# 44 unit-matrix products on TensorE in the routing of a two-block network, and the last norm computed half by half on three engines

## The reference

```python
logits = jnp.einsum('bsd,de->bse', h, w_router).astype(jnp.float32)
aff = jax.nn.softmax(logits, axis=-1)
gate, idx = lax.top_k(aff.transpose(0, 2, 1), cap)      # cap = 128
xe = jax.vmap(lambda hb, ib: hb[ib])(h, idx)
...
```

```python
h = h + jnp.einsum('bsf,fd->bsd', jax.nn.silu(gate) * up, w_down[l])
return rms_norm_2(h, final_norm_w)
```

## Time and profile before

| | us |
|---|---|
| median of 3 runs | 3355.08 |
| lowest and highest | 3353.43, 3356.0 |
| the profiled execution's own time | 3356.99 |
| its span from first to last instruction | 3355.2 |
| TensorE matmuls busy | 3210.2 (96%) |
| VectorE busy | 2716.5 (81%) |
| ScalarE busy | 1782.5 (53%) |
| GpSimd busy | 692.0 (21%) |
| mean granted TensorE clock | 0.985 |

### The profile page before, as it was taken

How to read it: one execution, slowest core, us unless ns; L and a number is a source line. 1 busy time by engine, 2 the same in 40 slices (tenths; PEclk the granted TensorE clock), 3 DMA queues, 4 the chain that set the end, 5 groups by cost and what they waited for, 6 DMA issues and landing times. The chain is left out here.

```text
span 3355.2 us, 43403 instructions
## 1 busy us (share of the span) xinstructions
PE 3210.2 (96%) x15284; PEld 2590.3 (77%) x15284; DVE 2716.5 (81%) x2579; ACT 1782.5 (53%) x1911; POOL 692.0 (21%) x551
## 2 busy tenths in 40 slices
PE   7999996999999999999699999999998999999998
PEld 4859874888888785897488888888777878888786
DVE  7988887999989798888789888886744598888667
ACT  4254534887887524544378888863233353334223
POOL 0213100111111020320011111104453033233233
PEclk9999997999999999999899999999999999999999
DMA  5120165999999412005499999962110434444953
GB/s 201 38 96 16 36 214 217 394 409 404 410 403 410 181 51 87 22 8 192 184 377 397 395 393 396 391 261 82 47 38 16 154 113 151 142 166 148 372 233 137
DMA packets 143517, 703.06 MB, mean 210 GB/s; under 512 B 19376, under 2 KB 28080, under 8 KB 90672
## 3 DMA queue, kind: packets, MB, share of 16 engines
q1 hardware_dynamic: 132240, 664.65, 51.3%
q0 software_dynamic: 8928, 32.51, 3.6%
q10 hardware_dynamic: 2240, 4.46, 0.3%
HBM read 608.75 MB, written 85.46 MB: 207 GB/s over the span
## 5 line engine op out<-in xcount | busy, mean ns | idle before, releaser
L2212 DVE TENSOR_TENSOR ex_lo_layer<-mix_layer,ex_hi_layer 128x2048 fp32r<-128x2048 f32 x128 | 291.6, 2289 | 23.0 <-ACT ex_hi_layer L2140 21.3
L2212 DVE TENSOR_TENSOR ex_lo<-mix,ex_hi 128x2048 fp32r<-128x2048 f32 x128 | 289.5, 2285 | 12.5 <-ACT ex_hi L2140 10.8
L2140 ACT CAST ex_hi<-mix 128x2048 fp32r<-128x2048 f32 x126 | 239.8, 1912 | 77.3 <-DMA mix<-w_experts_dram 33.5
L2140 ACT CAST ex_hi_layer<-mix_layer 128x2048 fp32r<-128x2048 f32 x126 | 240.6, 1911 | 65.2 <-PE psum L2054 50.9
L3199 PE MATMUL psum<-ff_rest,w_hi 128*128 128x512 f32 x776 | 241.2, 392 | 8.6 <-DVE ff_ev L3477 2.8
L2052 PE MATMUL psum<-ex_hi_layer,xe_hi_layer 128*128 128x512 f32 x512 | 201.4, 393 | 1.0 <-DVE xe_lo_layer L2217 1.0
L2052 PE MATMUL psum<-ex_hi,xe_hi 128*128 128x512 f32 x512 | 201.3, 393 | 1.0 <-DVE xe_lo L2217 1.0
L2054 PE MATMUL psum<-ex_hi_layer,xe_lo_layer 128*128 128x512 f32 x512 | 200.1, 391 | 0.0
L2054 PE MATMUL psum<-ex_hi,xe_lo 128*128 128x512 f32 x512 | 200.1, 391 | 0.0
L2053 PE MATMUL psum<-ex_lo,xe_hi 128*128 128x512 f32 x512 | 199.8, 390 | 0.0
L2053 PE MATMUL psum<-ex_lo_layer,xe_hi_layer 128*128 128x512 f32 x512 | 199.8, 390 | 0.0
(11 more groups left out here) (800 smaller groups left out, 8822.2 us busy)
## 6 DMA issues: line engine op xcount, KB each, us to landing
mix<-w_experts_dram SPq DMA_DIRECT2D x128, 1024.0 KB, 12.1
mix_layer<-w_experts_dram SPq DMA_DIRECT2D x128, 1024.0 KB, 7.1
first_w<-w_experts_dram SPq DMA_DIRECT2D x64, 1024.0 KB, 9.3
hid_rows<-x SPq DMA_DIRECT2D x71, 512.0 KB, 3.7
ex_raw<-w_experts_dram SPq DMA_DIRECT2D x32, 1024.0 KB, 10.8
ex_raw_layer<-w_experts_dram SPq DMA_DIRECT2D x32, 1024.0 KB, 7.5
first_w<-w_in_dram SPq DMA_DIRECT2D x42, 512.0 KB, 3.3
ff_rest<-hid_rows SPq DMA_DIRECT2D x13, 1536.0 KB, 14.4
```

The costliest lines, as they stand in the source:

```text
L2140: act.copy(hi[j % PARTS][:], raw[j % RAW][:]).then_inc(w_hi, 1)
L2212: dve.tensor_tensor(lo[j % PARTS][:], raw[j % RAW][:], hi[j % PARTS][:].bitcast(F32), ALU.subtract).then_inc(w_lo, 1)
```

## The change

In `route`, TensorE gets 44 products of the unit matrix into bank 5 behind the last transpose of the rows and ahead of the wait for `place_done`. In the last stage the results `u2` and `u3` of the last unit go to PSUM banks 2 and 3. ScalarE multiplies tiles 0, 1 and the first half of tile 2 with the gain early; tile 7 is squared in two halves, the second first. TensorE finishes the sum of the first half before it begins the second. ScalarE writes the inverse of each half twice, into PSUM and into `sq_sum`. VectorE multiplies 5 tiles of the first half and 6 of the second, GpSimd the 3 and 2 others, and SP writes them out in an order that interleaves both.

```diff
+GAINED_TILES = (3, 2)
...
                                 mm = pe.transpose(banks(2 + 4 * b)[:, k * P:(k + 1) * P], h[:, k, blk * P:(blk + 1) * P], ident)
                             mm.then_inc(row_turned[b], 1)
+                        keep_busy(pe, 5, 44)
                         pe.wait_ge(place_done, 4)
...
+                def u2_of(n):
+                    return bank(2) if n == n_units - 1 else u2_row
+                def u3_of(n):
+                    return bank(3) if n == n_units - 1 else u3_row
...
                     @block.sync
-                            for k in range(DT):
-                                sp.wait_ge(normed, DT * half + k + 1)
+                            gained = GAINED_TILES[half]
+                            own = list(range(gained, DT))
+                            order = [k for n in range(len(own)) for k in own[n:n + 1] + ([n // 2] if n % 2 and n // 2 < gained else [])]
+                            order += [k for k in range(gained) if k not in order]
+                            for k in order:
+                                if k < gained:
+                                    sp.wait_ge(normed_too, half * GAINED_TILES[0] + k + 1)
+                                else:
+                                    sp.wait_ge(normed, half * (DT - GAINED_TILES[0]) + k - gained + 1)
                                 sp.dma_start(out[k * P:(k + 1) * P, at], x[:, k, at]).then_inc(written, 16)
...
                     @block.gpsimd
                         for tile in (DT - 4, DT - 3):
                             add_square(pool, tile)
+                        pool.wait_ge(out_gained, 3)
+                        for half, at in enumerate(halves):
+                            pool.wait_ge(inverted_too, half + 1)
+                            for k in range(GAINED_TILES[half]):
+                                pool.tensor_tensor(x[:, k, at], x[:, k, at], sq_sum[:, at], ALU.mult).then_inc(normed_too, 1)
...
                     @block.tensor
                         pe.wait_ge(sq_added, DT - 3)
-                        for half in range(2):
-                            pe.matmul(bank(sum_bank + half), ones, sq_sum[:, half_of(half)], start=True, stop=False)
+                        pe.matmul(bank(sum_bank), ones, sq_sum[:, first_half], start=True, stop=False)
                         pe.wait_ge(sq_done, DT - 1)
                         pe.matmul(bank(sum_bank), ones, square_of(DT - 2)[:, first_half], start=False, stop=False)
-                        pe.wait_ge(sq_done, DT)
+                        pe.wait_ge(sq_done, DT + 1)
                         pe.matmul(bank(sum_bank), ones, square_of(DT - 1)[:, first_half], start=False, stop=True).then_inc(r["summed"], 1)
+                        pe.matmul(bank(sum_bank + 1), ones, sq_sum[:, second_half], start=True, stop=False)
                         pe.matmul(bank(sum_bank + 1), ones, square_of(DT - 1)[:, second_half], start=False, stop=False)
-                        pe.wait_ge(sq_done, DT + 1)
+                        pe.wait_ge(sq_done, DT + 2)
                         pe.matmul(bank(sum_bank + 1), ones, square_of(DT - 2)[:, second_half], start=False, stop=True).then_inc(r["summed"], 1)
...
                     @block.scalar
+                            if n == n_units - 1:
+                                act.wait_ge(sq_done, 3)
+                                for k, at in ((0, slice(0, S)), (1, slice(0, S)), (2, first_half)):
+                                    act.activation(x[:, k, at], x[:, k, at], ACT.Copy, scale=out_gain[:, k:k + 1]).then_inc(out_gained, 1)
...
+                        act.wait_ge(dn_done, dn_at(n, "x2"))
+                        square(DT - 1, (second_half,), 1)
                         act.wait_ge(dn_done, dn_at(n, "x21"))
-                        square(DT - 1, (slice(0, S),), 1)
+                        square(DT - 1, (first_half,), 1)
                         act.wait_ge(dn_done, dn_at(n, "x12"))
                         square(DT - 2, (second_half,), 1)
-                        inverse_norms(act, r, sum_bank, sq_sum)
+                        for half, at in enumerate(halves):
+                            act.wait_ge(r["summed"], half + 1)
+                            act.activation(sq_sum[:, at], bank(sum_bank + half), ACT.Ln, bias=EPS, scale=1.0 / D).then_inc(r["logged"], 1)
+                            act.wait_ge(r["logged"], half + 1)
+                            act.activation(bank(sum_bank + half), sq_sum[:, at], ACT.Exp, scale=-0.5).then_inc(r["inverted"], 1)
+                            act.wait_ge(r["inverted"], half + 1)
+                            act.activation(sq_sum[:, at], sq_sum[:, at], ACT.Exp, scale=-0.5).then_inc(inverted_too, 1)
...
                     @block.vector
-                            dve.tensor_tensor(u2, bank(4 * (n % 2) + 1), p1, ALU.add)...
+                            if n == n_units - 1:
+                                dve.wait_ge(dn_done, dn_at(n - 1, "x12"))
+                            dve.tensor_tensor(u2_of(n), bank(4 * (n % 2) + 1), p1, ALU.add)...
...
-                        for half in range(2):
-                            at = half_of(half)
+                        for half, at in enumerate(halves):
                             dve.wait_ge(r["inverted"], half + 1)
-                            for k in range(DT):
-                                dve.scalar_tensor_tensor(out=x[:, k, at], in0=x[:, k, at], scalar=out_gain[:, k:k + 1], in1=sq_sum[:, at],
+                            for k in range(GAINED_TILES[half], DT):
+                                dve.scalar_tensor_tensor(out=x[:, k, at], in0=x[:, k, at], scalar=out_gain[:, k:k + 1], in1=bank(sum_bank + half),
```

More of the change, by code:

```diff
@@ L2937, in mix_and_feed_forward @@
                 so = split_tensors("so", DT, ctx, parts)
-                p1, u3, sil1, u2 = (ev[:, i, :] for i in range(4))
+                p1, u3_row, sil1, u2_row = (ev[:, i, :] for i in range(4))
+                def u2_of(n):
+                    return bank(2) if n == n_units - 1 else u2_row
+                def u3_of(n):
+                    return bank(3) if n == n_units - 1 else u3_row
                 sil = ev[:, 2:4, :].rearrange("p a n -> p (a n)")
@@ L2955, in mix_and_feed_forward @@
                 normed, written = sem("ff_normed"), sem("ff_written")
+                out_gained, inverted_too, normed_too = (sem("ff_" + n) for n in ("out_gained", "inverted_too", "normed_too"))
                 slot_in = [sem(f"ff_slot_in{i}") for i in range(SLOTS)]
@@ L3311, in gate_2 @@
                             act.wait_ge(ev_done, ev_at(n, "g2s"))
-                            act.activation(u2, u2, ACT.Silu).then_inc(silu2, 1)
+                            act.activation(u2_row, u2_row, ACT.Silu).then_inc(silu2, 1)
                         def block_hi(g):
@@ L3476, in take_u2 @@
                                 dve.wait_ge(dn_done, dn_at(n - 1, "u12"))
-                            dve.tensor_tensor(u2, bank(4 * (n % 2) + 1), p1, ALU.add).then_inc(ev_done if n < FFT else dn_done, 1)
+                            if n == n_units - 1:
+                                dve.wait_ge(dn_done, dn_at(n - 1, "x12"))
+                            dve.tensor_tensor(u2_of(n), bank(4 * (n % 2) + 1), p1, ALU.add).then_inc(ev_done if n < FFT else dn_done, 1)
                         def take_u3(n):
@@ L3484, in take_u3 @@
                                 dve.wait_ge(dn_done, dn_at(n - 1, "x2"))
-                            dve.tensor_tensor(u3, bank(4 * (n % 2) + 1), p1, ALU.add).then_inc(ev_done if n < FFT else dn_done, 1)
+                            dve.tensor_tensor(u3_of(n), bank(4 * (n % 2) + 1), p1, ALU.add).then_inc(ev_done if n < FFT else dn_done, 1)
                         def gate_in(n):
@@ L3500, in up_second @@
                             dve.wait_ge(ev_done, ev_at(n, "u3"))
-                            dve.tensor_tensor(hid[n % 2][:, second_half], bank(4 * (n % 2) + 2), u3, ALU.add).then_inc(ev_done, 1)
+                            dve.tensor_tensor(hid[n % 2][:, second_half], bank(4 * (n % 2) + 2), u3_row, ALU.add).then_inc(ev_done, 1)
                         def up_first(n):
                             dve.wait_ge(prod, prod_at(n, 5))
-                            dve.tensor_tensor(hid[n % 2][:, first_half], u3, bank(4 * (n % 2) + 3), ALU.subtract).then_inc(ev_done, 1)
+                            dve.tensor_tensor(hid[n % 2][:, first_half], u3_row, bank(4 * (n % 2) + 3), ALU.subtract).then_inc(ev_done, 1)
                             dve.wait_ge(ev_done, ev_at(n, "c21"))
@@ L3511, in gate_in_2 @@
                             dve.wait_ge(ev_done, ev_at(n, "u2"))
-                            dve.tensor_tensor(u2, bank(4 * (n % 2) + 2), u2, ALU.add).then_inc(ev_done, 1)
+                            dve.tensor_tensor(u2_row, bank(4 * (n % 2) + 2), u2_row, ALU.add).then_inc(ev_done, 1)
                             dve.wait_ge(ev_done, ev_at(n, "g2"))
```

(6 more changed lines are left out.)

## The result

The changed kernel takes 3365.81 us in the median of 8 runs (3364.02 to 3366.87), the kernel before 3354.92 in the same session (3353.37 to 3358.32). The ratio is 1.0032, with a 95% interval from 1.0021 to 1.0042: slower by 0.3%. The forecast was 3363.4, with a range from 3360.5 to 3367.5.

What follows compares the result with a forecast made beforehand. TensorE's matmuls, busy 96% of the span, were taken as the bound, so work ahead of its needed work is paid in full. +11.1 - 1.2 + 1.0 - 2.6 = +8.3 us on 3355.08 gave 3363.4, range 3360.5 to 3367.5.

Steps and rivals of the forecast that it cites:

- The stream's length: Routing, both layers: 44 products last 18.9 us against a wait of 13.2 or 13.3, sum +11.1 us.
- Lateness less what comes back: Routing: places 5.6 and 5.5 us late, less full-clock gains at the block's end and in small records, -1.2 both layers.
- The restart of the experts: First expert products: more idle time during the gather lets the clock fall earlier, +1.0 us for both layers (0 to +3.6).
- The last stage: Final multiplications and output: VectorE's first multiplication starts earlier and the end follows, -2.6 us (-1.5 to -3.3).
- the faster supply: Last stage: GpSimd multiplying 5 of 16 tiles supplies outputs faster, priced at 0, hidden by the output DMAs.
- `u3` starts as before: Last stage: u3 starts at 3332.65 as now, since it waits for TensorE.
- a delay of the squares: Last stage, ScalarE: three early gain multiplications take 2.5 us and make the squares 0.8 late.
- the farthest corners of the bounds: Whole forecast: bounds +6.2 to +12.6, the range said to take them without farthest corners, +5.4 to +12.4.
- that the products fit: Rival, routing wait: 88 records take less than 13.2 us, no place transpose late, 3351.3 us; chance 0.05.
- the clock pays back half of its half-clock time: Rival, routing: the 17 us half-clock stretch disappears, each layer gains 8.5 us less 5.6 lateness, 3346.7 us; chance 0.02.
- fell to half clock: Rival, routing: 44 products take some 38 us, 19 more in each layer, about 3401 us; chance 0.02.
- new delay: Rival, last stage: GpSimd and VectorE block each other, output is fed unevenly, the 2.6 us are lost, 3366; chance 0.08.

Runs made afterwards that it cites:

- the last stage alone: The changed kernel without the 44 products of each layer: 3355.06 us beside 3355.98 for the kernel before, ratio 0.9995.
- the 30 products: The changed kernel with 30 products in place of 44 in the wait for the places: 3354.04 us, ratio 0.9994.
- VectorE alone: The changed kernel without the 44 products, all 16 final multiplications on VectorE, no early gains on ScalarE: 17.1 us from last unit to end in one profiled execution.
- `u2` and `u3` in SBUF: The changed kernel without the 44 products, u2 and u3 of the last unit back in SBUF: 18.9 us from last unit to end in one profiled execution.
- 88 products: The changed kernel with 88 products in place of 44 in each layer: 3404.80 us, ratio 1.0143.
- the products alone: The kernel before with the 44 products of each layer and nothing else: 3365.68 us, ratio 1.0028.
- the three kernels with 16 products: New last stage, 16 products in place of 10 during the gather: with no products in the wait 3353.03 us, with 30 3350.64, with 30 and VectorE multiplying alone 3349.30.
- the last pair: 30 products in the wait and 16 during the gather: on the kernel before 3352.25 us, with the new last stage, all multiplications on VectorE, 3349.30.
- in the first: The pair of the kernel before, 3355.98 us, and the changed kernel without its 44 products, 3355.06 us.
- the fastest kernel: The changed kernel with 30 products in the wait, 16 during the gather, all 16 final multiplications on VectorE, no early gains: 3349.30 us, ratio 0.9986.

## Why the prediction was right

The sign and the mechanism held, and the size to within 2.6 us: +8.3 us were forecast and 10.9 measured. Term by term, with the distances in the profiled executions counted from the end of the row transposes:

- *The stream's length.* 88 x 0.215 = 18.9 us forecast, 19.09 measured. The transpose of the places starts 18.93 us behind the row transposes in either layer, instead of 13.16 and 13.30: 5.8 and 5.6 late, where 5.6 and 5.5 were forecast.
- *Lateness less what comes back.* Forecast 5.6 - 0.6 = 5.0 in layer 0; the index copy comes 21.70 us behind the row transposes (566.05 - 544.35) instead of 16.74 (561.49 - 544.75), 4.96 later. What comes back is 0.8 us a layer (2.77 us from the transpose of the places to the index copy instead of 3.59): the 0.45 at the block's end as taken, and 0.37 in the small records where 0.15 was taken. In layer 1 the first expert product comes 31.34 us behind the transposes (1690.90 - 1659.56) instead of 26.33, 5.0 later.
- *The restart of the experts.* Forecast +1.0 for both layers. In layer 0 the half-clock stretch over the products grew from 3.4 to 5.7 us, which costs an estimated 1.1, about half of the difference; in layer 1 it stayed at 3.4. That the size fits is in part luck, since this stretch differs between executions. The working calls it hardly ever shorter than 3.4 us; but it is absent in 4 of the 16 layers with 10 products (layer 1 of the last stage alone, of the 30 products and of VectorE alone; layer 0 with `u2` and `u3` in SBUF), with TensorE idle ahead of the rows there too. With 44 or 88 products it is there in all 6 layers. Filling that gap, too, takes the stretch away, which the forecast had not asked.
- *The last stage.* Forecast -2.6; measured 20.3 - 17.8 = 2.5 in the traces, and here two errors cancel. The sum waited for GpSimd's additions, as forecast (0.74 us of idle time ahead of L3273), but these ended 0.6 us later than before and not 0.3 (ScalarE's three multiplications took 2.81 us and not 2.5, and 0.15 us lie between the two additions). The first multiplication is 2.3 us earlier and not 2.6. The 0.2 to 0.3 us missing there came from the faster supply, which the working had priced at 0. The working also says that `u3` starts as before because it waits for TensorE: in the earlier trace rows it follows `u12` at once, so it waited for VectorE, and with `u12` short it started 0.5 us earlier. That changed nothing, as tile 7 had slack. The 0.8 us that ScalarE's early multiplications cost was in the working as a delay of the squares, but I let it pass as part of the step instead of asking what the division was good for; it was good for 0.2 us.

Together the traces give 4.96 + 5.0 + 1.1 - 2.5 = 8.6 us, against 8.3. The measured medians differ by 10.9 and the two profiled spans by 9.5. What no term of the forecast covered is the start of the down projection, where TensorE waits twice, for a DMA and then for VectorE, whose own work had waited for the transfer `x<-x_rows` of 8.7 us (timeline, first the kernel before, then the changed one; windows below):

```profile
3132.22 1.19 PE L3199 MATMUL psum<-ff_rest,w_hi 128*128 128x512 f32 x2 [2.44 <-DMA ff_rest<-hid_rows]
3146.11 0.70 PE L3199 MATMUL psum<-ff_rest,w_hi 128*128 128x512 f32 x2 [2.00 <-DVE ff_ev L3477]
...
3142.34 0.70 PE L3220 MATMUL psum<-ff_rest,w_hi 128*128 128x512 f32 x2 [2.43 <-DMA ff_rest<-hid_rows]
3156.22 1.19 PE L3220 MATMUL psum<-ff_rest,w_hi 128*128 128x512 f32 x2 [3.41 <-DVE ff_ev L3512]
```

```profile
3131.90:3135.30 3.40, 3.08 (x7) 2.48 (x8) 1.88 (x3) 0.00 (x0) 1.57 (x1) 0.50 1.03 425
...
3155.30:3162.00 6.70, 5.78 (x14) 4.56 (x15) 4.84 (x8) 0.00 (x0) 1.97 (x2) 0.51 1.03 422
```

In the kernel before the clock is at half for 3.4 us behind the first wait. TensorE is slower there and then waits less behind it (2.00 us instead of 3.41), so that the second wait still ends 13.9 us behind the first, as in the changed kernel, and it costs nothing. In the changed kernel it is at half for 6.8 us behind the second wait, where TensorE's products are all that follows. From the end of that wait to the end of the last unit it is 190.7 us, against 188.8 before and 188.1 with the products alone, whose clock is full behind both waits. This closes the sum: the second wait ends 10.1 us later than before (3156.22 and 3146.11), then 1.9 are lost, and the last stage gives 2.5 back, 9.5 in all. The 10.1 are 1.0 less than the terms of the two layers, which add up to 11.1; 0.4 of it is that the row transposes of layer 0 ended earlier, the rest isn't traced.

It also shows where the stage's 2.5 us went between the profiled executions of the products alone and of the changed kernel (spans 3364.1 and 3364.7; medians 3365.68 and 3365.81): 2.6 us were lost in this stretch. Whether the half clock behind the second wait comes with the new last stage or by chance is open. This part of the program is the same in all kernels. In the kept profiles, one execution each, it is there for 3.4 or 6.8 us with the new last stage in the changed kernel, the last stage alone, and the three kernels with 16 products. It is absent with the new stage in the four others (30 products; 88 products; `u2` and `u3` in SBUF; VectorE alone), and with the old stage in all three. The stage's gain shows as 2.95 of an expected 3.2 in the last pair, and as 0.9 of 2.6 in the first.

One sentence of the working is wrong by its own numbers: the range is said to leave out the farthest corners of the bounds, but its lower end, +5.4, lies below the lower bound of +6.2. The measured +10.9 is above both.

The rivals: that the products fit is refuted by 0.217 a record. The Trainium skill, "TensorE: Matmul & The Clock Gate", section "Back-to-back issue gap", with its isolated gap of an estimated 109 ns for 256 columns, holds for none of these f32 records; the measurement decides. That the clock pays back half of its half-clock time is refuted by the 30 products (1.0 us for two stretches of 17). The stream never fell to half clock. The last stage showed no new delay beyond the 0.3 us of GpSimd's additions.

## What to carry to other kernels

Measure the filler: take one product's cost in the very form used (type, columns, clock) from the trace, and multiply before comparing with the wait; past the wait every product is paid on the path, 0.44 us each here. Half clock costs only where TensorE's work is on the path: 17 us of it in the wait for the places were worth 0.8 us a layer, 3.4 us ahead of a wait for VectorE nothing, and 6.8 us behind that wait 1.9. So a wait is worth filling to its end when long work of TensorE follows at once, as behind the gather, and hardly when other engines' work follows. When transfers are as slow as the engine that feeds them, start the first one earlier, and don't divide the feeding.

## What was not expected of the hardware

- What filling the gaps is worth is small beside the spread, and the medians don't agree on how it adds up. With the new last stage 30 products in the wait gave 1.0 us, 16 while the gather runs gave 2.0, both together 4.4 (3355.06 to 3350.64, in two sessions). With the old last stage both together gave 2.7 (3354.91 to 3352.25, in one session). So that both give more than the sum of the parts is not shown.
- The clock behind the same wait differs between executions. At the start of the down projection it was at half for 3.4 us behind the first wait in the kernel before, for 6.8 us behind the second in the changed kernel, and behind neither with the products alone. Runs of the kernel before spread by up to 6.7 us within a session. One of the eleven runs of the fastest kernel took 3361.01 us with a mean granted clock of 0.942, where the ten others have 0.991 to 0.993.
- An addition of two SBUF operands took 2.64 us beside GpSimd's addition, where the same one from PSUM took 0.68. GpSimd's first addition took 2.40 as it does without the conflict, so that VectorE alone lost there; the second, beside `x2`, took 2.64 and so lost 0.24 itself.
